# Eight-head attention with outputs made by channel on two column halves of TensorE, and turned back to rows

## The reference

```python
s = einsum('bnqhgd,bnkhd->bnhgqk', qb, kb) * dh ** -0.5      # blocks of 128 queries, slabs of 384 keys
m = maximum(max(where(mask, s, NEG_INF), axis=-1), sink)
e = exp(s - m)
denom = sum(e, axis=-1) + exp(sink - m)
o = einsum('bnhgqk,bnkhd->bnqhgd', e, vb) / denom
```

## Time and profile before

| | |
|---|---|
| median of 3 runs | 2886.36 us (2885.7 to 2887.22) |
| the profiled execution | 2883.64 us, its span 2881.8 us |
| mean granted clock of TensorE | 0.962 |
| PE busy | 2665.8 us (93%) |
| PEld busy | 2240.7 us (78%) |
| DVE busy | 1676.5 us (58%) |
| ACT busy | 1495.7 us (52%) |
| POOL busy | 936.0 us (32%) |
| chain that ended last | PE 78%, DMA 7%, issue 6%, DVE 5%, ACT 3% |
| products of the windowed heads (L1856, values `v_swa`) | 728.9 to 1059.0 us from the span's start |

### The profile page before, as it was taken

The page is one execution under the profiler, slowest core; times in us unless marked ns, Lnnn a source line. Parts: engine busy times, 40 slices in busy tenths (PEclk is TensorE's granted clock), DMA queues, the critical chain, the costliest instruction groups (busy, mean ns, idle before and its releaser), DMA issues.

```text
span 2881.8 us, 44599 instructions
## 1 busy us (share of the span) xinstructions
PE 2665.8 (93%) x13970; PEld 2240.7 (78%) x13971; DVE 1676.5 (58%) x2955; ACT 1495.7 (52%) x2750; POOL 936.0 (32%) x755
## 2 busy tenths in 40 slices
PE   3899999999999978999999799469999999999968
PEld 3788888999888866888888588458888888888853
DVE  6566777555777765454521334567765635375856
ACT  5555767766555544344422322246765635365856
POOL 5555556566222213344443111001111111111215
PEclk7999999999999988999999899779999999999988
DMA  7122222111000023343432534268987846386997
GB/s 256 55 61 67 67 61 67 33 30 30 23 20 14 14 69 122 134 132 130 135 115 79 206 146 148 100 231 326 358 293 266 309 146 233 146 302 246 389 387 328
DMA packets 191176, 451.91 MB, mean 157 GB/s; under 512 B 36174, under 2 KB 86390, under 8 KB 189004
## 3 DMA queue, kind: packets, MB, share of 16 engines
q1 hardware_dynamic: 172044, 389.46, 38.2%
q0 software_dynamic: 14400, 52.44, 4.9%
q10 hardware_dynamic: 4608, 8.39, 0.8%
HBM read 380.01 MB, written 70.21 MB: 156 GB/s over the span
## 4 chain that ended last, share of the span: by engine, by line
PE 78%; DMA 7%; issue 6%; DVE 5%; ACT 3%; POOL 1%; SPq 0%; DVEq 0%; ACTq 0%; POOLq 0%
PE bank L1783 19%; PE bank L2006 13%; PE bank L1890 6%; PE O_ps L1856 5%; PE bank L1934 4%; DMA sb_w_in<-in_w_gate_up 4%; PE S_ps L2017 3%; PE E_ps L2017 3%; PE S_ps L1890 3%; PE E_ps L1890 3%; PE E_ps L1822 2%; PE S_ps L1837 2%; PE S_ps L1839 2%; PE S_ps L1934 2%; PE O_ps L1901 1%
## 5 line engine op out<-in xcount | busy, mean ns | idle before, releaser
L772 POOL TENSOR_TENSOR sb_h_lo<-sb_hT,sb_h_hi 128x512 fp32r<-128x512 f32 x256 | 379.6, 1505 | 480.8 <-ACT sb_h_hi L910 480.8
L2006 PE MATMUL bank<-sb_gu,sb_x_hiT 128*128 (+1 forms) x1568 | 494.0, 396 | 10.9 <-DVE sb_x_loT L1670 7.8
L1783 PE MATMUL bank<-sb_w_hi,sb_h_hi 128*128 128x384 f32 x1024 | 382.2, 373 | 5.6 <-POOL sb_h_lo L772 5.5
L2006 PEld LDWEIGHTS bank<-sb_gu,sb_x_hiT 128*128 128x128 f32 x1568 | 293.2, 189 | 74.0 <-issue 10.6
L1783 PE MATMUL bank<-sb_w_hi,sb_h_lo 128*128 128x384 f32 x1024 | 344.6, 337 | 0.0
L1783 PE MATMUL bank<-sb_w_lo,sb_h_hi 128*128 128x384 f32 x1024 | 343.7, 336 | 0.0
L1656 DVE TENSOR_TENSOR sb_gu<-sb_w_in,sb_gu 128x1024 f32 (+1 forms) x256 | 300.8, 1219 | 61.2 <-ACT sb_gu L1166 58.4
L828 POOL TENSOR_TENSOR sb_g_lo<-sb_g_raw,sb_g_hi 128x1408 fp32r<-128x1408 f32 x64 | 212.4, 3340 | 337.7 <-ACT sb_g_hi L1041 337.7
L1166 ACT ACTIVATE sb_gu<-sb_w_in 128x1024 f32 (+1 forms) x256 | 257.1, 1059 | 101.0 <-DMA sb_w_in<-in_w_gate_up 80.3
L2006 PE MATMUL bank<-sb_gu,sb_x_loT 128*128 (+1 forms) x784 | 307.5, 392 | 0.0
L1783 PEld LDWEIGHTS bank<-sb_w_hi,sb_h_hi 128*128 128x128 f32 x1024 | 193.2, 189 | 63.7 <-issue 59.8
(11 more groups left out here) (381 smaller groups left out, 5990.1 us busy)
## 6 DMA issues: line engine op xcount, KB each, us to landing
sb_w_in<-in_w_gate_up SPq DMA_DIRECT2D x256, 512.0 KB
sb_w_in<-in_w_expert_down SPq DMA_DIRECT2D x128, 512.0 KB
sb_g_raw<-in_w_gb SPq DMA_DIRECT2D x64, 704.0 KB, 4.1
sb_late_w<-in_w_ada SPq DMA_DIRECT2D x64, 256.0 KB, 2.8
sb_yp<-y_d SPq DMA_DIRECT2D x16, 1024.0 KB, 26.3
sb_w_raw<-in_w_qkv SPq DMA_DIRECT2D x112, 96.0 KB, 2.1
sb_x_round<-in_x SPq DMA_DIRECT2D x4, 2048.0 KB, 9.3
sb_wada<-in_w_ada SPq DMA_DIRECT2D x8, 1024.0 KB, 5.1
```

Source lines behind the costliest of these rows:

```text
L772: nc.gpsimd.tensor_tensor(h_lo[c][:, ks], tile_src(g, T, ks), h_hi[c][:, ks].bitcast(F32), ALU.subtract).then_inc(sem("h_lo_ready"), 1)
L1783: last = nc.tensor.matmul(bank[c][:, 0:PASS_COLS].rearrange("p (a m) -> p a m", a=1), x[c][:, k, :], w[:, ds(row + k, 1), :], start=(k == ...
L2006: last = nc.tensor.matmul(PS[j][:].rearrange("p (a n) -> p a n", a=1), x[:, k, :], gu[:, ds(gu_row(e, part, k), 1), j * DE:(j + 1) * DE], ...
```

## The change

The products of the windowed heads change operands: the values (64 columns) are the weights, the transposed probabilities (128 columns) stream, and the output has channels on partitions, head h of the pair on partitions 64h to 64h + 63. The loop goes over blocks first and heads inside, so that neighbours lie on different column halves. The output is then copied from `O_ps` to a new tile `o_turn` by ScalarE, turned back to queries on partitions by a transpose on TensorE into columns 384 to 511 of the first bank of `S_ps`, and divided by VectorE from there. Unit 0's copy stands on ScalarE between the two evictions of `E_ps`, its transpose on TensorE behind the transposes of unit 1 and its division at the end of VectorE's step. Unit 1's copy, transpose and division stand in the next step: the copy as ScalarE's first instruction, the transpose behind projection row 3, the division as VectorE's first work. The loop gets one more step, and `rden` one tile a unit.

```diff
+    O_COLS = slice(384, 512)
+    def second_pair(T):
+        return unit(3, T - 4, 1) if 3 * TILES_PER_GROUP <= T - 4 < STEPS else None
...
 ScalarE
+        def take_turned(n):
+            act.wait_ge(sem("pv_done"), n + 1)
+            wait(act, sem("o_turned"), n - SWA_T0)
+            nc.scalar.activation(o_turn[:], O_ps[:, 0:P], ACT.Copy).then_inc(sem("o_taken"), 1)
         def step(T, c, gs, loads):
+            if second_pair(T) is not None:
+                take_turned(second_pair(T))
             if gs[0] is not None:
                 raise_tile(T + 1, 1 - c, gs[0])
...
             if g3 == 3:
+                take_turned(unit(3, T - 3, 0))
                 probs_T(1)
...
 VectorE
+        def share(n, u, row, esk_u):
...
+            dve.wait_ge(sem("o_turned"), n - SWA_T0 + 1)
+            src = S_ps[:, 0, O_COLS].rearrange("p (h m) -> p h m", h=2)
+            nc.vector.tensor_tensor(row[:, :, 0:HD], src, rb, ALU.mult).then_inc(sem("o_done"), 1)
         def step(T, c, gs, loads):
+            if second_pair(T) is not None:
+                share(second_pair(T), 1, o_row[c][1], esk[c][1])
...
+                if g3 == 3 and u == 1:
+                    share(unit(3, T - 3, 0), 0, o_row[1 - c][0], esk[1 - c][0])
...
 TensorE
+        def turn_output(n, scores):
+            pe.wait_ge(sem("o_taken"), n - SWA_T0 + 1)
+            pe.wait_ge(sem("masked"), scores)
+            pe.wait_ge(sem("o_done"), n)
+            nc.tensor.transpose(S_ps[:, 0, O_COLS], o_turn[:], ident[:]).then_inc(sem("o_turned"), 1)
...
+            if second_pair(T) is not None:
+                turn_output(second_pair(T), unit(3, min(T - 3, STEPS - 1), 1) + 1)
             if g1 is not None:
                 pe.wait_ge(sem("rot_done"), T)
...
+                if g3 == 3 and u == 1:
+                    turn_output(unit(3, T - 3, 0), unit(3, min(T - 2, STEPS - 1), int(g2 is None)) + 1)
...
+                    if u == 0 and second_pair(T) is not None:
+                        pe.wait_ge(sem("o_done"), second_pair(T) + 1)
...
+                        wait(pe, sem("o_taken"), n - SWA_T0)
                         for j in range(nj):
+                            for h in range(2):
+                                last = nc.tensor.matmul(O_ps[h * HD:(h + 1) * HD, 0:P], v_swa[:, t + j, :], eT[:, h, j * P:(j + 1) * P],
+                                                        start=(j == 0), stop=(j == nj - 1))
```

More of the change, by code:

```diff
@@ L195, in body @@
     esk = [[m2(f"esk{c}{u}", [P, 2]) for u in range(2)] for c in range(2)]
-    rden = m2("rden", [P, 2])
+    rden = [m2(f"rden{u}", [P, 2]) for u in range(2)]
     late_w = [m2(f"late_w{c}", [P, CHUNK]) for c in range(2)]
@@ L199, in body @@
     late_row = m2("late_row", [1, CHUNK])
+    o_turn = m2("o_turn", [P, P])
     assert m2.at <= top_start, (m2.at, top_start)
@@ L474, in straight @@
             step(T, T % 2, gs, T < STEPS - TT)
-        for T in range(STEPS + 3):
+        for T in range(STEPS + 4):
             straight(T)
+    O_COLS = slice(384, 512)
+    def second_pair(T):
+        return unit(3, T - 4, 1) if 3 * TILES_PER_GROUP <= T - 4 < STEPS else None
     JOBS = ([(0, "b", k) for k in range(4)], [(u, "a", k) for k in range(2) for u in range(2)], [(1, "b", k) for k in range(4)],
@@ L1383, in late_take @@
             ins.then_inc(sem("late_rows"), 1)
+        def share(n, u, row, esk_u):
+            total = rden[u]
+            den = row[:, :, HD + 1:HD + 2].rearrange("p h a -> p (h a)")
+            nc.vector.tensor_tensor(total[:], den, esk_u[:], ALU.add).then_inc(sem("den_step"), 1)
+            dve.wait_ge(sem("den_step"), 2 * (n - SWA_T0) + 1)
+            nc.vector.reciprocal(total[:], total[:]).then_inc(sem("den_step"), 1)
+            dve.wait_ge(sem("den_step"), 2 * (n - SWA_T0) + 2)
+            rb = total[:].rearrange("p (h a) -> p h a", a=1).broadcast_to([P, 2, HD])
+            dve.wait_ge(sem("o_turned"), n - SWA_T0 + 1)
+            src = S_ps[:, 0, O_COLS].rearrange("p (h m) -> p h m", h=2)
+            nc.vector.tensor_tensor(row[:, :, 0:HD], src, rb, ALU.mult).then_inc(sem("o_done"), 1)
         def step(T, c, gs, loads):
             g1, g2, g3 = gs[2], gs[3], gs[4]
+            if second_pair(T) is not None:
+                share(second_pair(T), 1, o_row[c][1], esk[c][1])
             if g1 is not None:
@@ L1434, in step @@
                         nc.vector.tensor_tensor(snk[c][u][:], negm, sink_bc[:, ds(head, 2)], ALU.add).then_inc(sem("max_ready"), 1)
[L1435 to L1438, removed]
+                if g3 is not None and g3 < 3 and u == 0:
+                    n = unit(g3, T - 3, u)
                     dve.wait_ge(sem("pv_done"), n + 1)
                     src = O_ps[:, 0:P].rearrange("p (h m) -> p h m", h=2)
[L1441 to L1450, removed]
+                    nc.vector.tensor_copy(o_row[1 - c][u][:, :, 0:HD], src).then_inc(sem("o_done"), 1)
+                if g3 == 3 and u == 1:
+                    share(unit(3, T - 3, 0), 0, o_row[1 - c][0], esk[1 - c][0])
             if gs[1] == 3 and g2 != 3:
@@ L1849, in step @@
                     pe.wait_ge(sem("eT_ready"), n + 1)
-                    wait(pe, sem("o_done"), n)
                     t = tile_of(S)
                     nj = KEYS[g3] // P
-                    for h in range(2):
+                    if g3 < 3:
+                        wait(pe, sem("o_done"), n)
+                        for h in range(2):
+                            for j in range(nj):
+                                v = v_dil[:, ds(t + j, 1), h * HD:(h + 1) * HD]
+                                last = nc.tensor.matmul(O_ps[:, h * HD:(h + 1) * HD].rearrange("p (a m) -> p a m", a=1), eT[:, h, j * P:(j + 1) * P], v,
+                                                        start=(j == 0), stop=(j == nj - 1))
+                    else:
+                        if n == SWA_T0:
+                            pe.wait_ge(sem("o_done"), n)
+                        wait(pe, sem("o_taken"), n - SWA_T0)
                         for j in range(nj):
-                            v = v_dil[:, ds(t + j, 1), h * HD:(h + 1) * HD] if g3 < 3 else v_swa[:, ds(t + j, 1), :]
-                            last = nc.tensor.matmul(O_ps[:, h * HD:(h + 1) * HD].rearrange("p (a m) -> p a m", a=1), eT[:, h, j * P:(j + 1) * P], v,
-                                                    start=(j == 0), stop=(j == nj - 1))
+                            for h in range(2):
+                                last = nc.tensor.matmul(O_ps[h * HD:(h + 1) * HD, 0:P], v_swa[:, t + j, :], eT[:, h, j * P:(j + 1) * P],
+                                                        start=(j == 0), stop=(j == nj - 1))
                     last.then_inc(sem("pv_done"), 1)
```

## The result

| | before | after |
|---|---|---|
| median | 2886.03 us | 2972.11 us (2968.93 to 2975.84) |
| ratio, 95% interval | | 1.0305 [1.0292, 1.0317] |
| profiled execution: span | 2881.8 us | 2968.7 us |
| mean granted clock | 0.962 | 0.948 |
| PE / DVE / ACT busy | 2665.8 / 1676.5 / 1495.7 us | 2696.7 / 1679.7 / 1511.7 us |

The change makes the kernel 3% slower; 2974 us had been forecast. In the changed kernel the lines of before have moved: the projection is L1808, the transposes of the rotated tile L1840 to L1842, those of the probabilities L1856, the scores L1877, the products L1903, the copy L1006, the turn L1817; the exponentials are L1034 and L1037, the eviction of the projection L992 and L999, the reduction L1457.

The account below looks back on a forecast made before the run. TensorE's chain was taken to bound the kernel. Wait less shorter products 47.0, clock 38.1 and last steps 3 made 88 us on 2883.6, 2971.7; with 2.7 for the median, 2974 us. Range 2925 to 2989.

Parts of the forecast that it names:

- The wait: TensorE before the second pair's turn: idle 1.93 us a step until ScalarE's copy behind the exponentials is done.
- X: Zero point of a step's forecast times: the end of a tile's projection on TensorE, 860.15 us in the profile before.
- The step without the clock: One step of the stage at full clock: 12.24 us against 10.56, 1.68 more, in 28 steps.
- the other waits that were put at nothing: Rotated tile's copies, first pair's scores, SyncE's store and weight pieces, ScalarE's added 0.55 us a step: no cost.
- the lower end: Products of a unit: pairs at the pace of a transpose, 6 x 0.11 = 0.64 us, against 0.95 taken.
- the wait less the shorter products: The 28 steps that turn a second pair and project: 28 x 1.68 = 47.0 us more.
- The clock: Granted clock falls to 0.50 in four of five of the 28 steps, 1.7 us each: 38.1 us more.
- the stall without falls: Rival: same TensorE idle time each step, but the clock stays up: 50 us more, 2936 us; chance 0.22.
- The last four steps: Steps without projection: copy and turn add some 1 us each, seven products get shorter: +3 us, between -2 and +8.
- the case of one after another: Rival: column halves do not run side by side, products 1.68 us a unit, no clock falls: 2957 us; chance 0.14.
- The case on the other side: Rival: copy ready when TensorE reaches the second pair's turn, step 10.12 us: 2874 us, some 2857 with 0.64-us products; chance 0.05.

Follow-up runs that it names:

- the wait alone: Kernel before plus one TensorE wait for the second pair's exponentials ahead of the rotated tile's transposes, no copy or turn: 2928.38 us, 1.0162 of before.
- The early copy: Changed kernel with ScalarE's copy of the second pair's output moved between the two exponentials of the same step: 2902.61 us, 1.0065 of before.
- the filled wait: Changed kernel plus eight unused matmuls on TensorE ahead of the second pair's turn: 2933.73 us, 1.0171 of before.
- the two matmuls: Changed kernel plus two unused matmuls on TensorE ahead of the second pair's turn: 2933.55 us, 1.0174 of before.
- the second experiment: Changed kernel, copy between exponentials, second pair turned into its own columns of the unused projection bank behind the rotated tile's transposes, divided later: 2868.01 us, 0.9945.

## Why the prediction was right

*What bounds the stage.* TensorE's chain and nothing else, as read from rows 1 and 2: every wait put on it came out in full (the wait alone, with 1.43 us of idle time, made a step 1.61 us longer), and without a wait the shorter pieces came out too (the own columns, 10.11 us a step).

*The wait.* The forecast was an idle time of 1.93 us, ending at X + 5.02, released by ScalarE's copy. The trace has 1.93 us, ending at 855.00 + 5.00, released by L1006. (Two errors cancel in where it begins: the products end 0.14 us sooner than forecast, and the projection rows behind them take 0.14 to 0.17 longer, as the kernel with its own columns shows.) The early copy shows that its place in the queue is the cause.

*The step without the clock.* 12.24 us were forecast; the steps of the changed kernel without a fall take 12.24, those of the filled wait 12.25. So the other waits that were put at nothing did cost nothing. Two sizes in that sum were off and cancel: the products take 0.81 us, not 0.95 (the nearest row, the scores' pairs scaled to 128 columns, gave 0.14 us a pair; the pairs start 0.11 apart, as the lower end had it), and the transposes behind them take 0.81, not 0.65, since the piece behind the column halves starts late. A pair in the trace of the changed kernel, two starts at once, and all twelve weight loads of that unit (two views):

```profile
851.62 0.33 PE L1903 MATMUL O_ps<-sb_eT,sb_v_swa 128*64 128x128 f32 x2
...
851.62 0.64 PEld L1903 LDWEIGHTS O_ps<-sb_eT,sb_v_swa 128*64 128x64 f32 x12 [0.25 <-issue]
```

47.0 us were forecast for the wait less the shorter products, and 46.5 are measured.

*The clock.* 38.1 us were forecast and 39 are measured: falls in some 25 of 28 steps instead of 22, at 1.6 us each instead of 1.7. That the clock falls was reasoned from rows; how often was a guess, and that 38 and 39 us lie so close is luck. The rows of before could not settle it. They had a gap of 1.44 us after which the clock stayed and one of 2.30 after which it fell (rows 6 and 7), and a gap of 1.58 us in every step, as the two matmuls show, would have made the second case, the stall without falls (2936), the true one: that case was a third of a microsecond of idle time away.

*The last four steps.* From the last projection to the first matmul of the next stage 41.8 us before (1029.1 to 1070.9) and 45.0 after (1114.4 to 1159.4): 3.2 us, 3 forecast.

*The rivals.* The columns do run side by side, so the case of one after another falls; a unit's twelve passes take 0.81 us with their weight loads, where one after another was worked out as 1.68. The trace does not agree with the rule of the Trainium skill that was weighed with it (TensorE: Matmul & The Clock Gate, Part 3, The mechanism: weight loads overlap running matmuls only where the row groups differ): all twelve loads lie in 0.64 us beside the passes. The case on the other side needed the copy to start before X + 2.8; the second experiment put it there, cleared the next wait too, and got 2868 (14.8 us under before), where 2874 to 2857 (12 to 29 under) had been worked out. With the drain at a change of mode that the Trainium skill states (TensorEngine Tiling (Array Packing), Key Properties) the trace agrees by the 0.14 to 0.17 us by which the piece behind the products is longer; no run parts a drain from another cause of it.

## What to carry to other kernels

Before an operation is put between two steps of a busy engine, look for its place in the queue of the engine that feeds it: the place of a copy of 0.25 us cost 66 us, because it stood behind exponentials whose input came 2.6 us later than its own, while its engine had been idle for 1.53 us just before. Then look at the next wait behind the one removed; here moving the copy gave most back, and only a place of its own for the result turned the loss into a gain. And price an idle gap on TensorE twice, once for itself and once for the clock that may fall in it.

## What the runs showed of the hardware that was not expected

Passes on different column halves run side by side even where they are not neighbours in the order. With all six passes of one head ahead of the six of the other, passes on one half 0.11 us apart would take 12 x 0.11 = 1.3 us if the second head began after the first; the unit took 1.07. Timeline of TensorE in that run, from one unit's start up to 860.50, 860.67, 860.70 and 860.85 us:

```profile
860.40 0.32 PE L1908 MATMUL O_ps<-sb_eT,sb_v_swa 128*64 128x128 f32 x1
...
860.40 0.54 PE L1908 MATMUL O_ps<-sb_eT,sb_v_swa 128*64 128x128 f32 x3
...
860.40 0.60 PE L1908 MATMUL O_ps<-sb_eT,sb_v_swa 128*64 128x128 f32 x4
...
860.40 0.71 PE L1908 MATMUL O_ps<-sb_eT,sb_v_swa 128*64 128x128 f32 x6
```

The first three passes have started after 0.27 us; at 0.11 us a pass one half alone would have a fourth at 0.38 and none further by 0.45, but by then six have started. So the second head's passes start while the first head still has passes to come, 0.27 us later than with neighbours on different halves (1.07 us instead of 0.81) but not last. The trace does not name a pass's head; this is read from the spacing. That each engine works through its queue in order, as said ahead of the prediction, holds for TensorE only with this exception. How far ahead TensorE looks was not tried.

What the clock costs here hangs on little idle time: 1.92 us a step gave falls in 25 of 28 steps, 1.58 us none in the profiled run, and matmuls that nobody uses made the kernel 35 us faster.
